# Experts' rows laid out in the order of work: input tiles of 128 rows that reach across experts, 22 and 21 instead of 32 and 32

## The chip, the core and the metric

One core of one Trainium2 chip runs the whole program. The metric is the device time in microseconds (us), a median over runs of one kernel. An expert's matrices are streamed from HBM for every use; nothing stays on the chip between the two layers.

## The reference, cut to what matters

The program is two transformer blocks of width 1024 on 1024 tokens. The change touches only the mixture of experts (MoE) that ends each of them. It is computed in float32:

```
logits -> one of 4 groups per token, then the top 2 of its 8 experts   # 2048 (token, expert) pairs
for each expert e, for its tokens x:
    y = (silu(x @ w_gate[e]) * (x @ w_up[e])) @ w_down[e]              # 1024 -> 512 -> 1024
out[token] += weight * y
```

There are 32 experts per layer, with 6 MB of weights each (gate, up and down of 2 MB).

## The kernel before

**Rooms.** How many tokens an expert gets is known only at run time, while the instructions are written beforehand. So the kernel ranks the experts by their counts on the chip and gives rank `r` a *room* of fixed size: `caps[r]` units of 32 rows, from a table `PROFILE`. Layer 0 has 88 units (2816 rows) in 31 rooms, layer 1 has 82 (2624 rows). What is over, and the expert of rank 31, goes through a small loop over 64 rows (`tensor_loop` and its likes; one pass of it runs here in each layer). `rooms(L)` makes the table of capacities and bases, from which VectorE works out each token's place (`vector_route`) and, through one-hot matmuls, the index table `xidx` that says which token lies in which row.

**Blocks.** A room is worked in blocks of 64 or 32 rows (`Plan.blocks`, in the order of `ORDER`). Layer 0 has 51, layer 1 has 46. For each block TensorE (PE) does gate and up together (L1914, eight steps over the contraction, the two in separate halves of the array's columns), the block before's hidden rows are turned (L1857), and the block before's down product follows (L1876). These stand in `tensor_experts.segment`.

**Tiles.** The rows that blocks read come in *tiles* of up to 128 rows (`Plan.tiles`). Per tile GpSimd (POOL) gathers the tokens' rows from HBM with one indirect DMA (`rows_in`, L1941), five tiles ahead (`XBUF = 5`); PE turns them with eight transposes (`turn`, L1846), VectorE (L1728) and ScalarE (L1800) copy them out of PSUM with four instructions each. The turn of the next tile stands in the middle of the first block of a tile:

```python
if off == 0 and t + 1 < tiles:
    turn(t + 1)
```

Before the change a tile covers rows of one room, or of two neighbouring rooms of odd size, so an expert with 64 rows has a tile of 64 rows for itself. Layer 0 then has 20 tiles of 64 rows and 12 of 128; layer 1 has 23 and 9. Gather slots without a token are marked as out of bounds and skipped.

**Weights.** The SyncE queue (SP) loads six pieces of 1 MB per expert (L2028, `sync_experts`) into 19 places (`homes`; 15 in layer 1). A piece waits until the block that used its place last is through. The loop's six pieces are issued between the experts, and the pieces that take over its places wait until the loop is done (`sync_loop_done`). The pieces' order and places depend only on rooms and blocks.

**Results.** Each block's product is written to `YE` in HBM (L1949). When all are through, `gpsimd_combine` gathers two rows of `YE` per token (L2178).

In the listing `Plan.__init__` builds order, blocks and tiles.

Of the kernel before, what the change touches and what calls it, by code (L numbers as in the profile page):

```python
# [27 lines left out]
def make_consts():  # L28
# [32 lines left out]
    for L in range(2):  # L61
        add(f"room{L}", rooms(L))
# [16 lines left out]

def rooms(L):  # L80

    r = np.arange(32)
    cap, base = np.full(32, 32), 32 * r
    for t in PROFILE[L]:
        cap, base = cap + 32 * (r < t), base + 32 * np.minimum(r, t)
    return np.concatenate([cap, base, 64 * (PLAN[L].places + 1) - cap - base])[None, :]


class Sig:


    def __init__(self, sem):
        self.sem, self.n = sem, 0
# [1506 lines left out]
Block = namedtuple("Block", "q at rows first tile off")  # L1600


class Plan:
# [1 line left out]


    def __init__(self, profile, firsts, before, homes):
        caps = [1 + sum(r < t for t in profile) for r in range(31)]
        base = [sum(caps[:r]) for r in range(31)]
        self.places = sum(caps) // 2  # L1610

        self.order, self.blocks, self.tiles, starts = [], [], [], []
        for r in firsts:
            g = [r, r + 1] if caps[r] % 2 else [r]
            assert base[r] % 2 == 0
            starts.append(len(self.order))
            at, end = base[r], base[g[-1]] + caps[g[-1]]
            t0 = len(self.tiles)
            self.tiles += [(u, 32 * min(4, end - u)) for u in range(at, end, 4)]
            for r in g:  # L1620
                u, e = base[r], base[r] + caps[r]
                while u < e:
                    n = 1 if u % 2 or e - u == 1 else 2
                    self.blocks.append(Block(len(self.order), u, 32 * n, u == base[r], t0 + (u - at) // 4,
                                             32 * ((u - at) % 4)))
                    u += n
                self.order.append(r)
        assert sorted(self.order) == list(range(31))
        self.ends = {}
        for n, row in enumerate(self.blocks):  # L1630
            self.ends[row.q] = n + 1
        self.loop_q = min(q for q in starts if q >= 26)
        self.b0, self.t0, self.w0 = (0, 0, [0] * HOMES) if before is None else (
            before.b0 + len(before.blocks), before.t0 + len(before.tiles), before.filled)
        self.place_pieces(homes)
# [38 lines left out]
PROFILE = ((23, 12, 6, 5, 5, 3, 3), (27, 11, 5, 3, 3, 1, 1))  # L1674
# [4 lines left out]
PLAN = [Plan(PROFILE[0], ORDER[0], None, HOMES_IN[0])]  # L1679
# [1531 lines left out]
```

How the kernel before makes its waits and increments, by code:

```python
def wait_sent(k, e, job):  # L246
    u, count = landed_by(job)
    e.wait_ge(k.s[f"d_sent{u}"].sem, count)
# [21 lines left out]
def vector_first_mods(k):  # L271
    V, s = k.nc.vector, k.s
    v, mod = mod_views(k), s["v_mod"]
    def rows(n):
        V.wait_ge(s["p_col"].sem, SUMS_DONE[n])
        got = k.ps[:, 4 + n, 0:128]
        if n == 0:
            V.wait_ge(s["d_gate"].sem, 128)
        if n < 2:
            V.tensor_tensor(v.rows[:, n, :], got, v.bias[:, n, :], ALU.add).then_inc(*mod.up())
            return
        V.scalar_tensor_tensor(v.rows[:, n, :], got, 1.0, v.bias[:, n, :], ALU.add, ALU.add).then_inc(*mod.up())
        V.wait_ge(mod.sem, mod.n)
        V.tensor_tensor(v.rows[:, n, :], v.rows[:, n, :], v.gain[:, n - 2, :], ALU.mult).then_inc(*mod.up())
    def columns(n):
        V.wait_ge(s["p_col"].sem, TURNS_DONE[n])
        V.tensor_copy((k.sh1, k.sc1)[n // 2][:, 4 * (n % 2):4 * (n % 2) + 4], k.ps[:, n, 0:128:32]).then_inc(*mod.up())
    rows(0)
    rows(1)
    columns(0)
    rows(2)
    columns(1)
    rows(3)
    columns(2)
    columns(3)
    V.wait_ge(mod.sem, COLUMNS_MADE)
    for h in range(2):
        for kk in range(5):
            x_ = k.hT[:, kk, 512 * h:512 * h + 512]
            i_ = V.tensor_scalar(x_, x_, k.sc1[:, kk:kk + 1], k.sh1[:, kk:kk + 1], ALU.mult, ALU.add)
        i_.then_inc(*mod.up())
    V.wait_ge(s["d_small"].sem, 112)
# [2 lines left out]
def scalar_first_mods(k):  # L308
    S, s = k.nc.scalar, k.s
    S.wait_ge(s["v_mod"].sem, COLUMNS_MADE)
    for h in range(2):
```

## Time and profile before

| | |
|---|---|
| median of 3 runs (lowest to highest) | 2941.55 us (2939.59 to 2944.01) |
| the profiled execution's own time | 2942.17 us |
| its span in the profile | 2941.0 us |
| MoE of layer 0, from its first matmul to its last | about 885 to 1455 us |
| MoE of layer 1 | about 2330 to 2891 us |

Two measures are read together. The busy time of PE says whether matmuls follow each other without a gap. The DMA share says whether the 16 DMA engines have work all the time; a share of about 1.0 means that the stream of weights can't go faster. Where PE is busy throughout and the DMA share falls below 1, the stream waits for PE to free places. The layer's weights are 192 pieces of 1 MB.

### The profile page before, as it was taken

The numbers are of one execution on the slowest core, as the hardware profiler recorded it, in microseconds if no ns is written. First come the engines' busy times: TensorE is split into PE (matmuls) and PEld (weight loads), VectorE is DVE, ScalarE is ACT, GpSimd is POOL, SyncE is SP. The second block draws the span as 40 slices with busy tenths as digits, with TensorE's granted clock in tenths as the row PEclk, the third lists the DMA queues.
The fourth block names the chain that finished last, engine by engine and source line by source line (L and its number), as shares of the span: only waits on it lengthen the run. The fifth ranks groups of instructions, "written<-read, shape, count | busy, mean of one in ns | idle before, by whom it ended". The sixth has DMA issues, their size and how long they took to land.

```text
span 2941.0 us, 36152 instructions
## 1 busy us (share of the span) xinstructions
PE 2657.5 (90%) x13778; PEld 1322.0 (45%) x13778; DVE 1128.0 (38%) x2869; ACT 670.2 (23%) x1612; POOL 394.2 (13%) x443
## 2 busy tenths in 40 slices
PE   5999999999968999999769998999899489999982
PEld 3466944444543344443335764555544334334431
DVE  3224927455251222222171114777843412222224
ACT  3115710000121111110050002656532211111111
POOL 1000000001001111111122111222610111111102
PEclk9999999999978999999879999999999799999996
DMA  8221014635149999998851111000000699999997
GB/s 304 114 79 58 2 51 164 200 129 200 38 179 389 403 389 359 399 395 348 327 202 47 43 43 29 30 30 30 15 31 29 240 397 388 383 361 372 358 413 292
DMA packets 207012, 607.57 MB, mean 207 GB/s; under 512 B 58928, under 2 KB 114488, under 8 KB 157560
## 3 DMA queue, kind: packets, MB, share of 16 engines
q1 hardware_dynamic: 150248, 540.17, 48.1%
q0 software_dynamic: 56592, 65.08, 6.7%
q8 instruction: 111, 1.82, 0.3%
q14 instruction: 61, 0.50, 0.0%
HBM read 559.24 MB, written 52.18 MB: 208 GB/s over the span
## 4 chain that ended last, share of the span: by engine, by line
PE 81%; DVE 7%; DMA 7%; issue 2%; SPq 2%; ACT 1%; POOL 0%; DVEq 0%; POOLq 0%; ACTq 0%
PE ps L1914 20%; PE ps L1876 9%; PE ps L1049 7%; PE ps L2577 6%; DMA R<-in_w_up 5%; PE ps L1370 4%; PE ps L543 4%; PE ps L1053 4%; PE ps L3077 3%; PE ps L2574 3%; PE ps L549 2%; PE ps L1846 2%; PE ps L1857 2%; PE ps L2852 2%; PE ps L855 1%
## 5 line engine op out<-in xcount | busy, mean ns | idle before, releaser
L1914 PE MATMUL ps<-R 128*64 128x512 f32 (+1 forms) x3480 | 645.6, 530 | 44.6 <-DMA R<-in_w_up 40.2
L1914 PEld LDWEIGHTS ps<-R 128*64 128x64 f32 (+1 forms) x3480 | 209.6, 129 | 332.3 <-issue 300.1
L1876 PE MATMUL ps<-R 128*64 128x512 f32 (+1 forms) x1744 | 278.1, 507 | 1.8 <-DVE R L1737 1.8
L1049 PE MATMUL ps<-R 128*128 128x512 f32 x512 | 225.6, 600 | 5.2 <-DMA R<-in_w_in 4.7
L1800 ACT ACTIVATE R<-ps,small 128x64 f32<-128x64 f32 (+1 forms) x256 | 87.0, 420 | 538.6 <-PE ps L1846 538.6
L1765 DVE TENSOR_TENSOR R<-ps,R 64x512 f32<-64x512 f32 (+1 forms) x97 | 59.9, 617 | 322.5 <-PE ps L1914 201.7
L1876 PEld LDWEIGHTS ps<-R 128*64 128x64 f32 (+1 forms) x1744 | 96.4, 126 | 168.2 <-issue 152.5
L1737 DVE COPY R<-ps 128x256 f32<-128x256 f32 (+1 forms) x97 | 38.0, 391 | 320.7 <-PE ps L1857 320.7
L1049 PEld LDWEIGHTS ps<-R 128*128 128x128 f32 x512 | 97.7, 192 | 129.0 <-issue 122.8
L1814 ACT ACTIVATE R<-ps 64x512 f32<-64x512 f32 (+1 forms) x97 | 52.4, 541 | 451.3 <-PE ps L1914 451.2
L1914 PE MATMUL ps<-XR,R 128*64 128x512 f32 (+1 forms) x392 | 132.2, 525 | 1.4 <-DVE R L1728 1.4
L1370 PE MATMUL ps<-R 128*128 128x512 f32 x256 | 113.5, 596 | 1.5 <-DVE R L1010 1.5
L3077 PE MATMUL ps<-R 128*128 128x512 f32 x256 | 113.7, 596 | 0.4 <-DVE R L2730 0.4
L543 PE MATMUL ps<-R 128*128 128x512 f32 x256 | 110.2, 592 | 0.0
L1949 POOL DMA_DIRECT2D YE<-R x49 | 39.7, 810 | 471.4 <-DVE R L1749 471.4
L1941 POOL DMA_INDIRECT R<-XN,xidx x52 | 53.6, 1030 | 342.6 <-DVE R L1522 324.2
L2577 PE MATMUL ps<-R 128*128 128x512 f32 x224 | 98.6, 592 | 0.0
L1728 DVE TENSOR_SCALAR R<-ps,small 128x64 f32<-128x64 f32 (+1 forms) x256 | 76.0, 359 | 40.8 <-PE ps L1846 40.0
L473 PE MATMUL ps<-cst,XR 128*128 128x128 f32 x256 | 38.0, 302 | 59.0 <-DVE XR L2267 35.0
L1026 ACT ACTIVATE XR<-ps 128x512 f32<-128x512 f32 x32 | 19.1, 597 | 305.3 <-PE ps L1049 305.3
L2852 PE MATMUL ps<-R,cst 128*128 128x512 f32 (+3 forms) x192 | 81.0, 504 | 1.2 <-DVE R L2767 1.2
L1857 PEld LDWEIGHTS ps<-cst,R 64*128 64x128 f32 x340 | 47.8, 208 | 69.4 <-issue 68.0
(376 smaller groups left out, 3973.9 us busy)
## 6 DMA issues: line engine op xcount, KB each, us to landing
R<-in_w_up SPq DMA_DIRECT2D x126, 1024.0 KB, 20.1
R<-in_w_down SPq DMA_DIRECT2D x117, 1024.0 KB, 21.9
R<-in_w_gate SPq DMA_DIRECT2D x107, 1024.0 KB, 22.2
R<-in_w_ada SPq DMA_DIRECT2D x40, 1024.0 KB, 5.5
XR<-in_w_gate SPq DMA_DIRECT2D x21, 1024.0 KB, 26.1
R<-in_w_in SPq DMA_DIRECT2D x7, 2048.0 KB, 13.6
R<-in_w_in SPq DMA_DIRECT2D x13, 1024.0 KB, 5.6
XR<-in_w_down SPq DMA_DIRECT2D x11, 1024.0 KB, 31.1
```

The source lines that it names most:

```text
L543: i_ = T.matmul(k.ps[:, b, :], wv[:, kk, 128 * a:128 * a + 128], toks, start=kk == 0, stop=kk == 7)
L1049: i_ = T.matmul(o, wv[:, kk, cols], k.hT[:, kk, tk], start=kk == 0, stop=kk == 7)
L1053: i_ = T.matmul(o, w4[:, g, cols], x4[:, g, tk], start=g == 0, stop=g == 3)
L1370: i_ = T.matmul(k.ps[:, n % 5, :], lhsT[:, m, 128 * i:128 * i + 128], wv[:, m, :], start=m == 0, stop=m == 7)
L1800: i_ = S.activation(v.xT[t % 2][:, 4 + kk, 0:n], k.ps[:, 3, 128 * kk:128 * kk + n], ACT.Identity, scale=scale[:, 4 + kk:5 + kk], bias=bias ...
L1857: i_ = T.transpose(k.ps[:, hidden_bank(b), 64 * kk:64 * kk + 64], h[:, kk, :], k.ident[0:64, 0:64])
L1876: i_ = T.matmul(k.ps[r * j:r * j + r, 5 + b % 2, 0:n], v.hT[b % 2][:, c:c + r], w[:, kk % 2, n * j:n * j + n], start=kk == 0, stop=kk == 3)
L1914: i_ = T.matmul(hidden_out(k.ps[P0 + r * j:P0 + r * j + r, b % 2, 0:n], r), x_, hidden_columns(w, r, j), start=kk == 0, stop=kk == 7)
L2574: i_ = T.matmul(o, right[:, kk, 128 * part.x:128 * part.x + 128], left[:, kk, :], start=first and kk == 0, stop=kk == 3, skip_group_check= ...
L2577: i_ = T.matmul(o, left[:, kk, :], right[:, kk, :], start=first and kk == 0, stop=kk == 3, skip_group_check=True)
L2852: i_ = T.matmul(z, k.C("nge"), lp[:, 0:N], start=False, stop=first and not diag, skip_group_check=True)
L3077: i_ = T.matmul(k.ps[:, mix_bank(n, a), :], v.oT[a][:, c, 128 * i:128 * i + 128], w[4 * a + c][:, 512 * h2:512 * h2 + 512], start=c == 0, ...
```

## The change

The bases of the rooms are no longer those of the ranks in a row, but those of the order in which the rooms are worked. So neighbours in time are neighbours in `xidx` as well, and a tile is simply the next 128 rows, across rooms. The cut is only at the loop: the rooms ahead of it are one run, those behind it another. Rooms, blocks, their order, the weights' order and places, the loop and the results' stores stay as they are, but for the addresses in `YE`.

```diff
@@ def rooms(L):
-    r = np.arange(32)
-    cap, base = np.full(32, 32), 32 * r
-    for t in PROFILE[L]:
-        cap, base = cap + 32 * (r < t), base + 32 * np.minimum(r, t)
+    P = PLAN[L]
+    cap = 32 * np.array(P.caps + [1])
+    base = 32 * np.array([P.base[r] for r in range(31)] + [2 * P.places])
@@ Plan.__init__
-        for r in firsts:
-            g = [r, r + 1] if caps[r] % 2 else [r]
...
-            at, end = base[r], base[g[-1]] + caps[g[-1]]
-            t0 = len(self.tiles)
-            self.tiles += [(u, 32 * min(4, end - u)) for u in range(at, end, 4)]
...
+        for begin, end in ((0, self.loop_q), (self.loop_q, 31)):
+            u0, t0 = at, len(self.tiles)
+            for q in range(begin, end):
+                r = self.order[q]
+                assert q not in starts or at % 2 == 0
+                self.base[r], u, at = at, at, at + caps[r]
+                while u < at:
+                    n = 1 if u % 2 or at - u == 1 else 2
+                    self.blocks.append(Block(q, u, 32 * n, u == self.base[r], t0 + (u - u0) // 4, 32 * ((u - u0) % 4)))
                     u += n
+            self.tiles += [(u, 32 * min(4, at - u)) for u in range(u0, at, 4)]
```

The change's lines are two fewer ahead of the experts' code, so L1846 of before is L1844 there, L1914 is L1912, L1941 is L1939.

**TensorE, a block in the middle of layer 0.** The block is the 27th of the layer (room 18, 64 rows); `R5` holds the turned rows, `R6` the hidden ones, `R1` the gathered ones, `R2` and `XR` weights. Before:

```order
L1914 MATMUL ps<-XR,R5 64x512
L1914 MATMUL ps<-R2,R5 64x512
L1857 MATMUL ps<-cst,R6 128x64 x4
L1846 MATMUL ps<-cst,R1 128x64 x8
L1914 MATMUL ps<-XR,R5 64x512
L1914 MATMUL ps<-R2,R5 64x512
```

The same block now:

```order
L1912 MATMUL ps<-XR,R5 64x512
L1912 MATMUL ps<-R2,R5 64x512
L1855 MATMUL ps<-cst,R6 128x64 x4
L1912 MATMUL ps<-XR,R5 64x512
L1912 MATMUL ps<-R2,R5 64x512
```

The turn of a tile of 64 rows is gone from this block; the block before it now turns a tile of 128 rows (`128x128 x8`) where it turned one of 64.

**GpSimd, the start of layer 0's MoE.** Each row is a DMA; the size is rows by columns gathered, and `L1968` is the loop's gather. Before:

```order
L1941 DMA R<-XN,xidx 64x1024 [waits v_rt,d_xn1,d_xn0]
L1941 DMA R<-XN,xidx 128x1024 x2
L1941 DMA R<-XN,xidx 64x1024
L1941 DMA g1b<-XN,xidx 64x1024
L1968 DMA R<-XN,xidx 64x1024
L1972 DMA SD<-cst 16x1x4
L1941 DMA R<-XN,xidx 64x1024 [waits p_xt]
L1949 DMA YE<-R 4x32x256 [waits v_yb]
L1941 DMA R<-XN,xidx 64x1024 [waits p_xt]
```

Now:

```order
L1939 DMA R<-XN,xidx 128x1024 [waits v_rt,d_xn1,d_xn0]
L1939 DMA R<-XN,xidx 128x1024 x3
L1939 DMA g1b<-XN,xidx 128x1024
L1966 DMA R<-XN,xidx 64x1024
L1970 DMA SD<-cst 16x1x4
L1939 DMA R<-XN,xidx 128x1024 [waits p_xt]
L1947 DMA YE<-R 4x32x256 [waits v_yb]
L1947 DMA YE<-acc 4x32x256 [waits v_yb]
L1939 DMA R<-XN,xidx 128x1024 [waits p_xt]
```

The five gathers ahead of the first block hold 640 slots where they held 448, and the sixth holds 128 where it held 64; the seventh stands one store later.

## Rows read from the trace of the kernel before

**Rows 1.** The page: busy time by engine; the chain that ended last, by engine.

```profile
PE 2657.5 (90%) x13778; PEld 1322.0 (45%) x13778; DVE 1128.0 (38%) x2869; ACT 670.2 (23%) x1612; POOL 394.2 (13%) x443
...
PE 81%; DVE 7%; DMA 7%; issue 2%; SPq 2%; ACT 1%; POOL 0%; DVEq 0%; POOLq 0%; ACTq 0%
```

**Rows 2.** Stretches: busy by engine (instructions), PE's granted clock, DMA share, GB/s.

```profile
911.00:1140.00 229.00, 229.00 (x1404) 91.24 (x1404) 50.62 (x115) 29.65 (x73) 29.12 (x33) 0.99 1.02 397
1145.00:1157.00 12.00, 12.00 (x58) 4.20 (x56) 1.80 (x3) 0.59 (x1) 0.86 (x1) 1.00 0.63 207
...
1341.00:1358.00 17.00, 17.00 (x132) 7.21 (x128) 4.02 (x9) 1.88 (x5) 1.63 (x2) 1.00 0.44 141
...
2373.00:2609.00 236.00, 228.29 (x1254) 91.95 (x1255) 52.23 (x120) 31.65 (x80) 31.90 (x35) 0.99 1.02 388
...
2637.00:2651.00 14.00, 14.00 (x72) 5.69 (x70) 3.32 (x8) 1.88 (x5) 1.24 (x2) 1.00 0.50 156
2651.00:2785.00 134.00, 134.00 (x910) 54.84 (x908) 30.59 (x71) 17.33 (x44) 18.51 (x21) 1.00 1.01 388
...
2790.00:2886.00 96.00, 80.09 (x443) 31.92 (x443) 17.35 (x44) 8.51 (x22) 6.76 (x9) 0.91 1.01 406
```

**Rows 3.** The chain in layer 0: start us, us, piece.

```profile
1082.26 0.89 PE ps L1846 x8
1083.15 3.58 PE ps L1914 x16
...
1094.22 3.58 PE ps L1914 x16
...
1190.04 3.58 PE ps L1914 x16
...
1201.11 1.09 PE ps L1846 x8
1202.20 3.58 PE ps L1914 x16
```

**Rows 4.** PE in time, layers 0 and 1, at waits: start us, us, [idle before].

```profile
910.77 4.53 PE L1914 MATMUL ps<-R 128*64 128x512 f32 x10 [9.71 <-DMA R<-in_w_up]
...
2373.10 5.35 PE L1914 MATMUL ps<-R 128*64 128x512 f32 x16 [4.43 <-DMA R<-in_w_up]
2518.55 3.65 PE L1914 MATMUL ps<-R 128*64 128x512 f32 x16 [0.58 <-DMA R<-in_w_up]
...
2608.96 5.48 PE L1914 MATMUL ps<-R 128*64 128x512 f32 x16 [6.10 <-DMA R<-in_w_up]
...
2868.76 3.56 PE L1914 MATMUL ps<-R 128*32 128x256 f32 x32 [2.35 <-DMA R<-in_w_up]
...
2884.62 2.02 PE L1914 MATMUL ps<-R 128*32 128x256 f32 x32 [1.42 <-DMA R<-in_w_up]
```

**Rows 5.** SP's DMA queue in time, around layer 1's loop.

```profile
2789.47 0.33 SPq L2028 DMA_DIRECT2D R<-in_w_gate  x1
...
2825.42 0.33 SPq L2028 DMA_DIRECT2D R<-in_w_up  x1
```

**Rows 6.** DMA queue of gathers and stores, 875 to 1457, then 2300 to 2897 us.

```profile
q0 software_dynamic: 25329, 20.08, 11.2%
...
q0 software_dynamic: 24304, 19.55, 10.9%
```

**Rows 7.** POOL in time, the first gather and the sixth tile's, layer 0.

```profile
876.46 1.27 POOL L1941 DMA_INDIRECT R<-XN,xidx  x1 [148.91 <-DVE R L1522]
...
886.73 0.99 POOL L1941 DMA_INDIRECT R<-XN,xidx  x1 [1.99 <-PE ps L1846]
```

**Rows 8.** VectorE's share of the copies in layer 0, by shape: busy us, mean ns.

```profile
L1728 DVE TENSOR_SCALAR R<-ps,small 128x64 f32<-128x64 f32 x80 | 22.0, 338 | 5.5 <-PE ps L1846 5.1
L1728 DVE TENSOR_SCALAR R<-ps,small 128x128 f32<-128x128 f32 x48 | 16.4, 404 | 15.0 <-PE ps L1846 15.0
```

**Rows 9.** A stretch at layer 0's first wait, columns as in rows 2.

```profile
906.00:916.00 10.00, 5.23 (x14) 1.72 (x16) 0.00 (x0) 0.00 (x0) 0.00 (x0) 0.50 1.02 376
```

More of the change, by code:

```diff
@@ L1607, in __init__ @@
     def __init__(self, profile, firsts, before, homes):
-        caps = [1 + sum(r < t for t in profile) for r in range(31)]
-        base = [sum(caps[:r]) for r in range(31)]
+        self.caps = caps = [1 + sum(r < t for t in profile) for r in range(31)]
         self.places = sum(caps) // 2
-        self.order, self.blocks, self.tiles, starts = [], [], [], []
-        for r in firsts:
-            g = [r, r + 1] if caps[r] % 2 else [r]
-            assert base[r] % 2 == 0
-            starts.append(len(self.order))
-            at, end = base[r], base[g[-1]] + caps[g[-1]]
-            t0 = len(self.tiles)
-            self.tiles += [(u, 32 * min(4, end - u)) for u in range(at, end, 4)]
[L1620 to L1625, printed above, removed]
+        groups = [[r, r + 1] if caps[r] % 2 else [r] for r in firsts]
+        self.order = [r for g in groups for r in g]
+        assert sorted(self.order) == list(range(31))
+        starts = [self.order.index(g[0]) for g in groups]
+        self.loop_q = min(q for q in starts if q >= 26)
+        self.base, self.blocks, self.tiles = {}, [], []
+        at = 0
+        for begin, end in ((0, self.loop_q), (self.loop_q, 31)):
[7 more added lines that the diff above has]
+                    self.blocks.append(Block(q, u, 32 * n, u == self.base[r], t0 + (u - u0) // 4, 32 * ((u - u0) % 4)))
                     u += n
-                self.order.append(r)
-        assert sorted(self.order) == list(range(31))
+            self.tiles += [(u, 32 * min(4, at - u)) for u in range(u0, at, 4)]
         self.ends = {}
@@ L1631, in __init__ @@
             self.ends[row.q] = n + 1
-        self.loop_q = min(q for q in starts if q >= 26)
         self.b0, self.t0, self.w0 = (0, 0, [0] * HOMES) if before is None else (
```

## The prediction

> **What bounds the kernel now.** I read the page first: PE is busy 90% of the span and makes 81% of the chain that ended last [rows 1]. A turn saved on PE can therefore be worth its time, but only where PE sets the pace, so the MoE stages have to be cut into stretches [rows 2]. The reader should hold two columns against each other. In layer 0, from 911 to 1140 us, PE is busy for all 229 us and the DMA engines are at 1.02 as well. Who leads shows where one of them lets go: from 1145 to 1157 and from 1341 to 1358 the DMA share falls to 0.63 and 0.44 while PE stays fully busy. The stream had filled every place and waited for PE. After the first wait, PE never waits for a weight in layer 0. So layer 0 is PE's from 910.77 us on, and before that it is the stream's: PE stands 9.71 us for a weight [rows 4].
>
> Layer 1 has three parts. Up to 2608.96 us the DMA share is 1.02 without a break, and PE is busy for 228.29 of 236 us [rows 2]; it waits for weights at 2373.10, 2518.55 and 2608.96, the last time for 6.10 us [rows 4]. There the stream leads. From 2609 to 2789 PE leads: it is never idle, and the share drops to 0.50 between 2637 and 2651 [rows 2]. Then SP issues pieces again from 2789.47 on [rows 5], the share is 1.01 to the end of the stage, and PE waits at 2868.76 and 2884.62 [rows 2, 4]. The tail is the stream's, but its start hangs on PE at 2789.
>
> **What goes from PE.** A turn costs what it adds to the distance between two like places of the chain. From 1083.15 to 1094.22 no turn lies between: 11.07 us. From 1190.04 to 1202.20 lies a turn of 128 rows: 12.16, so 1.09 us, which is also the length of the piece itself; the turn of 64 rows ahead of 1083.15 takes 0.89 [rows 3]. Twice the rows cost 1.22 times as much, so merging pays.
>
> *Layer 0.* After 910.77 us, 30 turns are left of the 32: 19 of 64 rows and 11 of 128, which is 19 x 0.89 + 11 x 1.09 = 28.9 us. Now 20 of 128 are left of 22: 21.8 us. **-7.1 us.** The first two turns, before and after, lie ahead of the weights' wait of 9.71 us and are worth nothing either way.
>
> *Layer 1.* What is saved before 2609 only lengthens the waits at 2518 and 2609. From there to 2789 there are 10 turns (6 of 64, 4 of 128: 9.7 us); now 7 (1 of 64, 6 of 128: 7.4 us). **-2.3 us**, which SP's issues after 2789.47 inherit and with them the whole tail. The four turns behind the loop become two (3.6 to 2.2 us); the waits at 2868 and 2884 absorb that.
>
> A rule of the skill speaks against all this. In the Trainium skill, "TensorE: Matmul & The Clock Gate", section "Back-to-back issue gap", the gap follows the moving columns: about 60 cycles for up to 64, 134 for 128. By that ratio of 2.2 a turn of 128 rows would cost 1.99 us beside 0.89, layer 0 would have 19 x 0.89 + 11 x 1.99 = 38.8 us before and 39.8 after, and the change would lose 1 us there. The trace's 0.89 and 1.09 [rows 3] disagree with it (its figures are for bf16), and the sum goes by the trace.
>
> **What it adds.** *Wider copies.* VectorE's four copies per tile take 404 ns each instead of 338 [rows 8]. They hide behind half a block, except at the first tile behind the loop, where PE waits for them: 4 x 66 ns = **+0.3 us** in layer 0; in layer 1 the tail's waits hide it.
>
> *Rows fetched earlier.* No slot is added over a layer, but five tiles of lookahead are 640 slots now. By the first weights' wait in layer 0, six tiles hold 768 slots instead of 512, and a seventh of 64 was issued at about 903 before: 192 to 256 slots more. How many carry a row? q0 moved 20.08 MB in layer 0 [rows 6]; 2816 + 64 stored rows of 4 KB are 11.8, so 8.3 MB or some 2020 rows were gathered from 2816 slots, 0.72. In layer 1 it is 19.55 - 11.0 = 8.5 MB from 2624 slots, 0.79. So 140 to 185 rows, 0.57 to 0.75 MB, go ahead of weights on engines that are full (share 1.02); at the 397 GB/s of rows 2 that is 1.4 to 1.9 us. I take **+1.7 us** for layer 0. The gathers are issued from 876 to 887 us [rows 7], in time to be ahead of the pieces that PE waits for at 910. The bounds are 0, if those pieces are ahead in their own queue anyway, and 256 full rows, 2.6 us. In layer 1, when the piece of 2608.96 is under way, the gathers stand at about tile 15 (1920 to 2048 slots) instead of 20 or 21 (1728 to 1792): some 220 x 0.79 = 170 rows more, 1.8 us at 388 GB/s. I take **+1.7 us**, bounds 0 and 2.7. Those rows are then missing from the traffic later; of them the last tile's (64 slots, about 50 rows) fell about 2780 to 2800, and without it the tail is **-0.5 us**.
>
> The Trainium skill, "DMA: Bandwidth & Descriptors", section "Queues, rings and completion order", says that each DMA engine takes packets from its queues in turn, so gathered rows do cut in ahead of queued weights. By that the upper part of the bounds applies; no row here shows the order of single packets.
>
> *Nothing else.* Table entries change, not the instructions that make them. A gather costs POOL about 1 us [rows 7]; there are 21 fewer. The gather of the tile five ahead still stands behind a wait for a turn, and the stores of results are queued behind it on POOL; that turn comes in the same block as before, so nothing is held longer. At the start the first tile lands later, since more of its slots carry rows; the 9.71 us that PE then waits anyway cover it.
>
> **The sum.** Layer 0: -7.1 + 0.3 + 1.7 = -5.1. Layer 1: -2.3 + 1.7 - 0.5 = -1.1. Together -6.2 us against the profiled execution's 2942.17 (span 2941.0 and 1.2 around it). That execution lies 0.6 us above the median of 2941.55, so the forecast for the median is 2941.55 - 6.2 = **2935.4 us**. A change of 0.2% (5.9 us) is about what a measurement of this kernel tells from none.
>
> **The rivals.**
> *The head start is free.* If the early rows ride beside the weights, both +1.7 vanish and the sum is -9.6: 2932. For it: q0 needs only 11% of the engines [rows 6]. Against it: the share is 1.02, so nothing is free. Chance 0.17.
> *The stream takes more back.* PE gets nearer to the stream in layer 0 as well. From 911 to 1140 PE gains about 3 us on a stream that is full all the time, and after 2651 it does so for 134 us. If new waits for weights eat half of the 7.1 and the 2.3, and the head start costs 2.6 and 2.7, the sum is -4.7 + 0.3 + 5.3 - 0.5 = +0.4: 2942. For it: the share of 1.01 to 1.02. Against: the idle stream at 1145 and 1341, which shows some us of slack. Chance 0.23.
> *The turn is priced by columns* (the rule above). With 1.99 us for a turn of 128 rows layer 0 gives +1.0 in place of -7.1; from 2609 to 2789 it is 6 x 0.89 + 4 x 1.99 = 13.3 us before and 0.89 + 6 x 1.99 = 12.8 now, so -0.5. With the other terms: 1.0 + 0.3 + 1.7 - 0.5 + 1.7 - 0.5 = +3.7, 2945. Rows 3 speak against it. Chance 0.02.
> *Slower: the clock.* At a wait PE's granted clock falls to the 1.2 GHz level: from 906 to 916 it is 0.50 [rows 9], with the wait of 9.71 us just before it [rows 4]. Work in such a stretch of 10 us takes 5 us longer. The waits at 910, 2373, 2518 and 2609 get longer. If each of two that PE's own part follows (910 and 2609) brings one such stretch more, that is +10 and 2945; with a third it is +15 and 2950. This case decides for slower when more than 6.2 + 5.9 = 12.1 us are lost, so from the third stretch on. Against it: the waits change by 2 us or less. Chance 0.08 for one stretch or more.
>
> **The numbers.** The forecast itself has a chance of 0.5, with a range of its own from 2933 to 2938. The range over all cases reaches down past the free head start and up past the stream's case: 2930.5 to 2943; some 0.07 lie below and 0.1 above. Faster by over 0.2% (below 2935.7) are 0.17 of the free head start and a little over half of the forecast's own case, 0.28, whose middle lies just under that bound, with 0.02 of the rest: 0.47. Slower by over 0.2% (above 2947.4) is most of the clock's case, 0.06. Within it: 0.47.
>
> **What the profile will show.** PE has 21 turns fewer, 168 transposes. If the theory is right, blocks without a turn stay 11.07 us apart and those with one are 12.16; no wait for a weight shows in layer 0 behind the first; the first waits end 1 to 2 us later than 910.77 and 2373.10; layer 0's MoE ends about 5 us earlier; and the wait at 2608.96 gets 1 to 2 us longer. The prediction is wrong if eight transposes of 128 rows take over 1.5 us, if waits for weights stand between 911 and the loop of layer 0, if the tail of layer 1 ends no earlier although SP's issues of 2789.47 do, or if a stretch of clock 0.50 shows that was not there.

## The result, and the profile after

The changed kernel takes **2912.84 us** (median of 4 runs, 2910.02 to 2918.0), beside 2942.78 us for the kernel before on the same chip (4 runs, 2939.59 to 2945.34). The ratio is 0.9901, with a 95% interval from 0.9883 to 0.9918: about 30 us less. The forecast was 2935.4 us with a range of 2930.5 to 2943. The time lies 18 us below that range.

The page of the profiled execution (span 2916.8 us, the slowest of the four runs), first the lines that answer to [rows 1], then the DMA queues:

```profile
PE 2643.1 (91%) x13610; PEld 1307.0 (45%) x13610; DVE 1110.6 (38%) x2785; ACT 648.3 (22%) x1528; POOL 374.1 (13%) x422
...
q1 hardware_dynamic: 150248, 540.17, 47.4%
q0 software_dynamic: 56256, 65.07, 6.5%
...
PE 81%; DVE 7%; DMA 6%; issue 2%; SPq 1%; ACT 1%; POOL 0%; DVEq 0%; POOLq 0%; ACTq 0%
```

The same two queues on the page of the kernel before (packets, MB, share of 16 engines over a span of 2941.0 us):

```profile
q1 hardware_dynamic: 150248, 540.17, 48.1%
q0 software_dynamic: 56592, 65.08, 6.7%
```

PE's busy time falls by 14.4 us (2657.5 to 2643.1) with 168 instructions fewer: 21 turns of eight transposes. That part was foreseen. The other part was not: q1, which holds the weights, moves the same 150248 packets and the same 540.17 MB, but in 47.4% of 2916.8 us (1382.6) instead of 48.1% of 2941.0 (1414.6). **The same packets took 32 us less of engine time.** A share is printed to 0.1%, so this is good to some 3 us.

Stretches after, columns as in [rows 2]:

```profile
911.00:1140.00 229.00, 229.00 (x1392) 89.66 (x1390) 48.15 (x103) 25.46 (x58) 27.52 (x31) 0.99 1.02 407
1145.00:1157.00 12.00, 12.00 (x60) 4.19 (x56) 1.80 (x3) 0.59 (x1) 0.86 (x1) 1.00 0.59 201
...
2360.00:2584.00 224.00, 224.00 (x1212) 86.06 (x1208) 47.62 (x99) 26.55 (x60) 25.14 (x28) 0.99 1.01 404
```

In layer 1, from its fourth block to the one at which the lead passed to PE (2609 before, 2584 now), the engines moved 388 GB/s before at a DMA share of 1.02 [rows 2]; now they move 404 at 1.01. The share was at its top both times and the rate was not. And PE, which was busy for 228.29 of 236 us there, is now busy for all 224.

PE in time at its waits for rows and weights, to be read against [rows 4]; the first line, the wait for the first tile's rows, answers to the 9.87 us of before:

```profile
887.59 1.97 PE L1844 MATMUL ps<-cst,R 128*128 128x128 f32 x8 [10.32 <-DMA R<-XN,xidx]
...
909.94 5.39 PE L1912 MATMUL ps<-R 128*64 128x512 f32 x12 [5.95 <-DMA R<-in_w_up]
...
2344.17 6.13 PE L1912 MATMUL ps<-R 128*64 128x512 f32 x16 [6.58 <-DMA R<-in_w_up]
...
2359.56 2.83 PE L1912 MATMUL ps<-R 128*64 128x512 f32 x6 [3.42 <-DMA R<-in_w_up]
...
2589.86 3.65 PE L1912 MATMUL ps<-R 128*64 128x512 f32 x16 [1.36 <-DMA R<-in_w_up]
...
2853.00 3.64 PE L1912 MATMUL ps<-R 128*32 128x256 f32 x32 [4.96 <-DMA R<-in_w_up]
```

The wait of 0.58 us at the block of 2518.55 is gone, and that of 6.10 us at 2608.96 too: the same block starts at 2584.24 without one. Over the program, the view of who waits for whom gives, first for before and then for after:

```profile
PE ps L1914 <- DMA R<-in_w_up: 40.2, 12, 9.7
```

```profile
PE ps L1912 <- DMA R<-in_w_up: 29.4, 9, 6.6
```

So 14.4 us less work on PE and 10.8 us less waiting for weights are 25.2 us, and the two profiled spans differ by 24.2. The turns themselves are as read before: blocks without one between them stay 11.08 us apart (1162.94 to 1174.02), and with one 12.16:

```profile
1162.94 3.58 PE ps L1912 x16
...
1174.02 3.58 PE ps L1912 x16
...
1185.09 1.09 PE ps L1844 x8
1186.18 3.58 PE ps L1912 x16
```

The time between like places, each less the same of before. The places are the first gate matmuls of the blocks that started at 910.8 (layer 0), 1447.8 (its last block), 2609.0 and 2789.5 (layer 1) before, and layer 1's first table matmul (2318.4). A second profile of the changed kernel (a0, below) stands beside it, since one profile scatters by some us:

| stretch | forecast | profile after | a0 |
|---|---|---|---|
| up to the end of layer 0's first wait for weights | +1.7 | -0.8 | -2.0 |
| from there to layer 0's last block | -6.8 | -9.9 | -10.2 |
| to layer 1's table | 0 | +0.6 | -0.5 |
| to the block of 2609 (weights led before) | +1.7 | **-14.6** | **-15.0** |
| to the block of 2789.5 (PE led) | -2.3 | -2.6 | -2.6 |
| to the end | -0.5 | +3.1 | -0.6 |
| sum | -6.2 | -24.2 | -30.9 |

Half of what came (15.0 of 30.9 us in a0) or more (14.6 of 24.2) lies in the one stretch in which nothing was to be gained. How far single profiles scatter is seen in e1 below, which does the same work as before and takes as long: its stretches differ from those of before by -1.3, -4.0, -0.1, +1.0, +0.8 and -1.5 us. So the second row is good to some 4 us, and the fourth stands far outside.

### The profile page after: what moved, and what is told of

Read it like the earlier page. It is cut to its first block, busy times and chain, and to the rows that moved or that the text cites. A ratio compares the mean times of both kernels' runs of the same rounds, so it can differ in the third digit from the quotient of the medians.

```text
span 2916.8 us, 35522 instructions
## 1 busy us (share of the span) xinstructions
PE 2643.1 (91%) x13610; PEld 1307.0 (45%) x13610; DVE 1110.6 (38%) x2785; ACT 648.3 (22%) x1528; POOL 374.1 (13%) x422
## 3 DMA queue, kind: packets, MB, share of 16 engines
q1 hardware_dynamic: 150248, 540.17, 47.4%
## 4 chain that ended last, share of the span: by engine, by line
PE 81%; DVE 7%; DMA 6%; issue 2%; SPq 1%; ACT 1%; POOL 0%; DVEq 0%; POOLq 0%; ACTq 0%
PE ps L1912 20%; PE ps L1874 9%; PE ps L1048 7%; PE ps L2575 6%; PE ps L1369 4%; PE ps L542 4%; DMA R<-in_w_up 4%; PE ps L1052 4%; PE ps L3075 3%; PE ps L2572 3%; PE ps L548 2%; PE ps L1855 2%; PE ps L2850 2%; PE ps L1844 1%; PE ps L854 1%
## 5 line engine op out<-in xcount | busy, mean ns | idle before, releaser
L1912 PE MATMUL ps<-R 128*64 128x512 f32 (+1 forms) x3480 | 641.5, 529 | 34.5 <-DMA R<-in_w_up 29.4
L1912 PEld LDWEIGHTS ps<-R 128*64 128x64 f32 (+1 forms) x3480 | 207.9, 129 | 321.8 <-issue 291.2
L1048 PEld LDWEIGHTS ps<-R 128*128 128x128 f32 x512 | 97.7, 192 | 129.2 <-issue 123.1
L1798 ACT ACTIVATE R<-ps,small 128x128 f32<-128x128 f32 (+1 forms) x172 | 64.7, 457 | 357.5 <-PE ps L1844 357.5
L1912 PE MATMUL ps<-XR,R 128*64 128x512 f32 (+1 forms) x392 | 130.6, 521 | 1.6 <-DVE R L1726 1.6
L1939 POOL DMA_INDIRECT R<-XN,xidx x35 | 37.8, 1081 | 341.3 <-DVE R L1521 325.3
L542 PEld LDWEIGHTS ps<-R 128*128 128x128 f32 x256 | 48.6, 190 | 61.2 <-issue 61.2
```

The lines of the kernel that those rows point to most:

```text
L542: i_ = T.matmul(k.ps[:, b, :], wv[:, kk, 128 * a:128 * a + 128], toks, start=kk == 0, stop=kk == 7)
L1048: i_ = T.matmul(o, wv[:, kk, cols], k.hT[:, kk, tk], start=kk == 0, stop=kk == 7)
L1798: i_ = S.activation(v.xT[t % 2][:, 4 + kk, 0:n], k.ps[:, 3, 128 * kk:128 * kk + n], ACT.Identity, scale=scale[:, 4 + kk:5 + kk], bias=bias ...
L1912: i_ = T.matmul(hidden_out(k.ps[P0 + r * j:P0 + r * j + r, b % 2, 0:n], r), x_, hidden_columns(w, r, j), start=kk == 0, stop=kk == 7)
```

## The experiments

**The theory.** The kernel before fetched 43 of its 64 tiles by gathers of 64 slots, which land in 64 of the 128 partitions; now one of 43 is. (The loop's own gather of 64 slots, one a layer, is the same in all kernels and not counted.) Such a gather slows the weights' packets that land beside it, a gather of 128 slots does not. **The rivals:** the new addresses do it; or TensorE's fewer turns do it alone, on the path.

Every kernel ran beside the kernel before on the same chip, and a ratio is to that. 2938.76 us was the time of before beside e1, e2, e3 and e5, 2940.68 beside a0, e4 and e6, and 2938.81 beside e7, e8 and e9.

### e1: the layout alone

The kernel before with the new addresses of the rooms, but its own 32 tiles a layer and its own gathers:

```
-    r = np.arange(32)
-    cap, base = np.full(32, 32), 32 * r
+    cap = 32 * np.array(P.caps + [1])
+    base = 32 * np.array([P.base[r] for r in range(31)] + [2 * P.places])
...
+                if q in starts:
+                    u0, t0 = at, len(self.tiles)
+                    over = at + sum(caps[x] for x in groups[starts.index(q)])
+                    self.tiles += [(u, 32 * min(4, over - u)) for u in range(u0, over, 4)]
```

> The rooms lie in the order of work as in the changed kernel, but tiles are cut per room as before: 32 and 32 tiles, 20 and 23 of them with gathers of 64 slots. Theory (a gather of 64 slots slows the weights' packets while it lands; one of 128 doesn't): as before, 2942 us within 0.2%, mean duration of a weights' packet in layer 1 about 334 ns as before. Rival (the new addresses in the index table and in the results' buffer make it faster): 2913 us.

2939.32 us, ratio 0.9999 (0.9989 to 1.0009). The addresses alone bring nothing that shows, and that rival is out.

### e2: the gathers alone

The kernel before, each tile of 64 rows fetched by a gather of 128 slots. The upper 64 slots' indices lie outside the table, so no row lands for them; some small VectorE instructions a layer write these indices.

```
-        at, n = P.tiles[t]
+        at, n = P.tiles[t][0], 128
...
+    up, got, n = k.xidx[64:128, :], k.ps[64:128, 1, :], PLAN[L].places
...
+    settle(V.tensor_scalar(up[:, 0:n], got[:, 0:n], 0.0, 3.0 * NO_ROW, ALU.mult, ALU.add))
+    for u in [u // 2 for u, n in PLAN[L].tiles if n == 128]:
+        V.tensor_scalar(up[:, u:u + 1], got[:, u:u + 1], float(NO_ROW), None, ALU.add).then_inc(*rt.up())
```

> The kernel before, with the same 32 and 32 tiles, turns and blocks, but every gather has 128 slots: where the tile has 64 rows, the upper 64 slots are marked out of bounds, so that the same rows move in the same number of DMAs. Theory (the gather's shape): the slow packets go, weights' packets at about 318 ns; 15 to 25 us less than before, so 2917 to 2927 us. Rival (fewer gathers, or fewer turns on TensorE, make the whole gain): as before, 2942 us.

2930.35 us, ratio 0.9965 (0.9953 to 0.9977): 8.4 us less, about half of what was expected, although the queue of weights gained all of it. The rows of those 43 tiles still land in partitions 0 to 63 alone, so the landing place by itself did not slow the stream; a gather of 64 slots did. Its line on the page (span 2930.8):

```profile
q1 hardware_dynamic: 150248, 540.17, 47.1%
```

That is 1380.4 us, as in the changed kernel. Its stretch of layer 1 shows where the rest went:

```profile
2373.00:2600.00 227.00, 226.15 (x1248) 89.81 (x1246) 52.16 (x120) 31.86 (x80) 30.83 (x33) 0.99 0.99 392
```

PE is busy for 226.15 of 227 us, and the DMA share is below 1 (0.99): the stream has room, and PE, which still makes all its turns, is what holds the stretch up. By the places of the table above, e2 gains 8.3 us in the stretch up to the block of 2609, where the stream led, and 0.3 us from layer 0's first wait to its last block, where PE leads. A faster stream alone is worth its time only up to where PE becomes the bound.

### e3, e4, e9: the turns alone, with more and fewer gathers of 64 slots

The changed kernel, its TensorE instructions untouched, with tiles of 128 rows fetched by two gathers of 64 slots: all of them (e3), every second one (e4), and every second one from the sixth on (e9). Shown is e4, cut; e3 has no `t % 2 == 1`, e9 has `and t > 4` behind it.

```
-        G.indirect_dma_start(v.xb[t % XBUF][0:n], None, k.XN[L],
-                             bass.IndirectOffsetOnAxis(ap=k.xidx[0:n, at // 2:at // 2 + 1], axis=0),
+        parts = [(0, 64), (64, n)] if n == 128 and t % 2 == 1 else [(0, n)]
+        for lo, hi in parts:
+            G.indirect_dma_start(v.xb[t % XBUF][lo:hi], None, k.XN[L],
+                                 bass.IndirectOffsetOnAxis(ap=k.xidx[0:hi - lo, (at + lo // 32) // 2:(at + lo // 32) // 2 + 1],
...
```

> The changed kernel with every tile of 128 rows fetched by two gathers of 64 slots, one into partitions 0 to 63 and one into 64 to 127; the turns stay those of the changed kernel. Theory (the shape): 44 and 41 such gathers where the kernel before had 20 and 23, each some 0.9 us of the stream: the stream leads everywhere, slower than the kernel before by 5 to 20 us, 2947 to 2962 us. Rival (fewer turns on TensorE make the gain): about 2913 us.

> The changed kernel, but every second tile of 128 rows is fetched by two gathers of 64 slots instead of one of 128 (22 gathers of 64 and 11 of 128 in layer 0, 21 of 64 and 10 of 128 in layer 1). TensorE's instructions are exactly those of the changed kernel, and the number of gathers of 64 slots is about that of the kernel before (20 a layer). Theory (a gather of 64 slots slows the weights' packets that land beside it, one of 128 does not; the turns alone are worth what the prediction said): 6 to 9 us faster than the kernel before, 17 to 20 us slower than the changed kernel. Rival (TensorE's fewer and wider turns bring the gain, or fewer rows of descriptors in all): as the changed kernel, about 26 us faster than before.

> The changed kernel, with tiles 5, 7, 9, ... of each layer fetched by two gathers of 64 slots, so that the five tiles ahead of the first weights stay whole: 35 gathers of 64 slots in the program instead of 1. If each costs the end time 0.75 us as in the other two, 25 us more than the changed kernel (about 2939). If a large part of the cost lies in the tiles ahead of the first weights (block 2 of layer 0 came 5 to 7 us later with them split), 12 to 16 us more.

| kernel | gathers of 64 slots for tiles | median us | ratio to before | q1's engine time, us (share x span) |
|---|---|---|---|---|
| changed | 1 | 2912.84 | 0.990 | 1382.6 |
| e9 | 35 | 2937.66 | 0.9994 (0.9984 to 1.0003) | 1415.9 (48.3% x 2931.5) |
| e4 | 43 | 2945.04 | 1.0016 (1.0006 to 1.0026) | 1422.2 (48.3% x 2944.6) |
| e3 | 85 | 2978.39 | 1.0139 (1.0116 to 1.0162) | 1455.3 (48.9% x 2976.1) |
| before | 43 | 2938.8 | 1 | 1414.6 |
| e2 | 0 | 2930.35 | 0.9965 | 1380.4 (47.1% x 2930.8) |

```profile
q1 hardware_dynamic: 150248, 540.17, 48.9%
...
q1 hardware_dynamic: 150248, 540.17, 48.3%
```

That is e3's line, then that of e4, which e9's page has too. The packets and bytes are those of before in each of them. Against a0, the changed kernel as it ran beside e4 (2913.5 us), e3's 84 more gathers cost 64.9 us, e4's 42 cost 31.5, e9's 34 cost 24.1: 0.77, 0.75 and 0.71 us of the end time each. The kernel before was 1.9 us faster beside e3 and e9 than beside a0, so their two prices may be some hundredths low. The rival is out, since TensorE's work is the same in all four. e3 was expected at 2947 to 2962 and came out at 2978; e4 was to be 6 to 9 us faster than before and is 4.4 slower; e9 came near the 2939 of its first case. The two misses have one side: in the changed kernel PE is so near to the stream that a slower stream is paid nearly in full (in e3 q1 takes 72.7 us more and the end comes 64.9 us later). The stretch of layer 1 in e3, over the same 224 us as the last row of after:

```profile
2360.00:2584.00 224.00, 194.25 (x1114) 75.96 (x1104) 39.93 (x85) 21.59 (x49) 29.92 (x33) 0.93 1.02 366
```

366 GB/s at a share of 1.02, and PE stands for 30 us. In e4 the saved turns are seen where PE leads (6.8 us less from layer 0's first wait to its last block, which is the forecast's term, though by one profile, good to some 4 us), but layer 0's block of 910.8 starts 5.2 us later, and the stretch up to the block of 2609 takes 4.6 us longer. e9 leaves the tiles ahead of the first weights whole, where e4 fetches tiles 1 and 3 by pairs of gathers, and its block is not late. That block in e4, then in e9:

```profile
915.94 4.53 PE L1912 MATMUL ps<-R 128*64 128x512 f32 x10 [11.55 <-DMA R<-in_w_up]
...
907.62 5.23 PE L1912 MATMUL ps<-R 128*64 128x512 f32 x16 [8.24 <-DMA R<-in_w_up]
```

### m1: the stream by itself

No part of the model: SP loads 252 pieces of 1 MB, and in six of seven phases POOL adds the same 0.52 MB of rows for every three pieces, in another form each time. It leaves out all computation, and its output is copied weights. It ran once.

```
g64       i_ = gather(x, 0, 64, ng % 4)          # twice
g128      i_ = gather(x, 0, 128, 4 + ng % 4)     # once
g128_low  i_ = gather(x, 0, 128, 8 + ng % 4)     # twice, upper 64 indices out of bounds
p64       i_ = G.dma_start(X[x][0:64, :], rows[64 * (ng % 16):64 * (ng % 16) + 64, :])      # twice
p128      i_ = G.dma_start(X[x][:, :], rows[128 * (ng % 8):128 * (ng % 8) + 128, :])        # once
g64_up    i_ = gather(x, 64, 64, ng % 4)         # twice
```

> No part of the model: a stream of weight pieces of 1 MB alone, in seven phases of 36 pieces, in which other transfers land beside it: none; two gathers of 64 slots for every three pieces; one gather of 128 slots; two gathers of 128 slots with the upper half of the slots out of bounds; two plain loads of 64 partitions; one plain load of 128 partitions; two gathers of 64 slots into partitions 64 to 127. Each gather of 64 slots is 0.25 MB of rows. Theory (what lands in 64 partitions only, lands through part of the ports and holds the weights' packets up): the phases with 64 partitions, gathers and plain loads alike, take 1.5 us more for each pair than the same bytes in 128 partitions; the phases with 128 slots take what their bytes need at the stream's own rate. Rival (it is a property of gathers, or of the out of bounds slots, not of the number of partitions): the plain loads of 64 and 128 partitions take the same. Rival (it needs TensorE's or VectorE's work beside it): no phase differs from its bytes.

Stretches inside the phases none, g64, g128, g128_low, p64, p128, g64_up (the last two columns are DMA share and GB/s):

```profile
20.00:75.00 55.00, 0.00 (x0) 0.00 (x0) 1.00 1.01 422
100.00:204.00 104.00, 0.00 (x0) 16.88 (x19) 1.00 1.02 343
212.00:308.00 96.00, 0.00 (x0) 10.87 (x11) 1.00 1.01 420
318.00:426.00 108.00, 0.00 (x0) 21.76 (x22) 1.00 1.00 393
440.00:560.00 120.00, 0.00 (x0) 11.20 (x22) 1.00 1.02 324
575.00:666.00 91.00, 0.00 (x0) 5.28 (x10) 1.00 1.01 419
684.00:800.00 116.00, 0.00 (x0) 18.68 (x20) 1.00 1.02 329
```

A transfer of 128 partitions leaves the rate at 419 to 422 GB/s, and two of 64 in its place take it down to 324 to 343, gather or plain load, lower half or upper. g128_low stands between (393), though its rows land in partitions 0 to 63 as those of g64 do. The share says 1.00 to 1.02 in all seven. POOL's issues follow the landing of every third piece, so their distance is the time for 3 pieces and 0.52 MB (3.67 MB in all, 8.7 us at 422 GB/s):

```profile
76.97 1.05 POOL L35 DMA_INDIRECT X<-in_x,idx  x1 [76.52 <-DMA W<-in_w_gate]
...
204.79 1.00 POOL L35 DMA_INDIRECT X<-in_x,idx  x1 [9.39 <-DMA W<-in_w_gate]
...
309.47 0.99 POOL L35 DMA_INDIRECT X<-in_x,idx  x1 [7.74 <-DMA W<-in_w_gate]
```

In g64 the twelve periods from 76.97 to 204.79 take 10.65 us each, in g128 those to 309.47 take 8.72. In the same way p64 takes 11.46, p128 8.79, g64_up 11.02 and g128_low 9.87. A transfer of 64 partitions thus costs the stream 0.97 us (gather, lower half), 1.15 (upper) or 1.33 (plain load, against p128) above its bytes. The rival that it needs work on other engines is out, and so is the one that it is a property of gathers. Slots out of bounds are a half cure here: such a gather still costs 0.6 us.

The packets in the traces show that this remainder is another thing. Each piece of weights comes as 128 packets of 8 KB, which take 314 ns on average with nothing beside them. Of them 35% take over 400 ns in g64, 36% in g64_up and 29% in p64, but none in the phase without rows and one of 4215 in g128. In g128_low none does from 318 to 366 us, and over the whole stretch it is 3%. So neither rows that land in half of the partitions nor two gathers in place of one hold the weights' packets up as 64 slots do. In the kernels the same count, of 49280 such packets, is 2678 before, 6677 in e3, 492 after and 546 in e2. How the packets of a transfer of 64 differ otherwise, and what the 0.6 us of g128_low are, no trace here shows.

The Trainium skill, "SBUF — State Buffer", section "Door 1: The DMA port swizzle", says that partitions 0 to 63 are reached through 8 of 16 ports only, and 64 to 127 through the other 8. The direction agrees with 343 against 420 GB/s and with the upper half behaving as the lower. As an estimate from that page, 0.262 MB at half of 420 GB/s take 1.25 us instead of 0.62, so 0.6 us more. The transfers of 64 partitions show 0.97 to 1.33, and the measurement decides. The halves alone do not explain them, since the rows of g128_low and e2 land in the same half. No run shows a port, so that the ports have a part in it is argued and not shown.

### e5: what a turn is worth now

The changed kernel, with the eight transposes of every third tile made twice: 15 turns more.

```
-            for kk in range(4):
+            for kk in 2 * list(range(4)) if t % 3 == 0 else range(4):
```

> The changed kernel, with every third tile turned twice (the second turn repeats the first), 7 x 1.09 = 7.6 us of TensorE's work more in layer 0 behind the first wait and 3.3 us more in the last part of layer 1: TensorE's time as before, gathers as in the changed kernel. Theory (TensorE's part as predicted, the rest of the gain is the stream's): 2921 to 2925 us, 8 to 11 more than the changed kernel. Rival (the whole gain is the stream's): 2913 us; rival (the whole gain is TensorE's): 2942 us.

2925.92 us, ratio 0.9956 (0.9937 to 0.9975), 12 to 13 us more than the changed kernel, a little above the 8 to 11 that were expected. Two of the 15 stand ahead of waits for the first weights; the other 13 cost 0.95 us each, near the 1.09 that a turn lasts. With the fast stream PE's time counts nearly everywhere, in layer 1 too: the stretch up to the block of 2609 takes 2.8 us longer than in the changed kernel's profile. So both rivals of e5, that the whole gain is the stream's or TensorE's, are out.

### e6, e7, e8 and a0: fewer rows fetched ahead

```
-XBUF, YBUF = 5, 6
+XBUF, YBUF = 3, 6        # e6, e7; 2 in e8
...
-        at, n = P.tiles[t]
+        at, n = P.tiles[t][0], 128        # e7 and e8: the last gather of 64 slots too
```

> The changed kernel with three buffers of gathered rows instead of five, so that three tiles instead of five are fetched at the start of a layer, ahead of or beside the first weights. The prediction took 1.7 us a layer for the rows that are fetched earlier. If that holds: 2 to 3 us faster than the changed kernel, and layer 1's first gate matmul 1 to 2 us earlier after its layer's start. Rival (these rows land beside the weights at no cost, since they come by gathers of 128 slots): as the changed kernel within 1 us; slower than it, if three buffers are too few and a tile's rows come late.

> The changed kernel itself, for comparison with the others on the same chip: 0.990 of the kernel before, as measured.

> The changed kernel with three buffers of rows, and layer 1's last tile of 64 rows fetched by a gather of 128 slots as well, so that no tile is fetched by 64 slots. Theory: that gather costs about 0.75 us of the end time as all others did (64.9 us for 84 of them, 31.5 us for 42), so 0.5 to 1 us less than with three buffers alone, 6 us less than the changed kernel. Rival: no difference from three buffers alone, since TensorE is the bound by then.

> The same with two buffers of rows. Theory (each tile fetched ahead of the first weights delays them by its bytes, 0.5 MB or 1.2 us): up to 1 us a layer less than with three. Rival: a tile's rows are asked for only when the tile two before it has been turned, and its turn waits for them: 1 us or more at many of 43 tiles, some 10 us and more in all.

a0, the changed kernel again: 2913.53 us, ratio 0.9912 (0.9895 to 0.9928). e6: **2908.05 us**, 0.9894 (0.9878 to 0.9911), 5.5 us below a0. The intervals of the two ratios overlap; the runs themselves hardly do (2907.05 to 2911.49 beside 2911.27 to 2915.97), so a gain of some us is likely and its size is not sure. Its first weights are there earlier; PE at both layers' first waits:

```profile
905.41 5.35 PE L1912 MATMUL ps<-R 128*64 128x512 f32 x16 [3.99 <-DMA R<-in_w_up]
...
2335.50 5.35 PE L1912 MATMUL ps<-R 128*64 128x512 f32 x16 [4.00 <-DMA R<-in_w_up]
```

905.41 beside 908.8 (a0) and 909.94 (after), so 3.4 to 4.5 us earlier; in layer 1, counted from its first table matmul, 2.7 us earlier than in a0. Two tiles of 128 slots are at most 1.05 MB, 2.6 us at 407 GB/s, so rows fetched ahead do cost their bytes or somewhat more: the prediction's term for a head start has the right kind. e7 (2909.72 us, 0.9894) shows no further gain from the last gather, whose 0.75 us lie below what four runs can tell. e8 (2910.23 us, 0.9886, 0.9866 to 0.9906) scatters from 2904.09 to 2915.68; the 10 us that its rival expected did not come, and whether two buffers are better or worse than three stays open. The best kernels of the study are thus the changed one with two or three buffers of rows, about 1.1% below before.

## Why the prediction was wrong

**The step that failed** is the reading of the DMA share. "There the stream leads" was right for layer 1 up to 2609, but the prediction took a share of 1.02 as a stream that cannot go faster (so it stands under "Time and profile before" too, and it is wrong), and priced the rows as bytes on it. It looked for a change of bytes (+1.7, +1.7, -0.5) and never asked at what rate they land. [rows 2] held the hint: 397 and 388 GB/s at 1.02, but 406 at 1.01 in the last stretch. The share counts the time in which a packet is under way, and a packet that is held up counts for longer. m1 shows 343 GB/s at 1.02 and 422 at 1.01, and e3 has 366 at 1.02 where after has 404 at 1.01. The gathers were counted ("there are 21 fewer", a cost on POOL only) and their slots too, but not how many slots one gather has.

**"What is saved before 2609 only lengthens the waits"** followed from it and fell with it: the turns were put at nothing there, and +1.7 us was added. That stretch gave 14.6 to 15.0 us: the stream became faster (e2 has 8.3 us of it with the turns of before), and so the turns saved on PE, which would have been worthless, counted as well. Neither part does much alone: the wide gathers without the turns bring 8.4 us (e2), the turns with 35 or 43 gathers of 64 slots bring 1.2 us, no more than the scatter, or lose 4.4 (e9, e4). Together they bring 27 to 30.

**Term by term.** Layer 0's turns: -7.1 forecast. e4, in which the stream is as burdened as before, shows -6.8 from the first wait to the last block, and the changed kernel -9.9 to -10.2; e1, with the turns of before, has -4.0 by scatter alone, so the term stands within what single profiles tell, and its price of 1.09 us and its count were right. Wider copies: 403 ns now beside the 404 of [rows 8], too small to be seen in the end. Rows fetched earlier: the first wait ends 0.8 to 2.0 us earlier and not 1.7 later. e6 shows that the bytes do cost at least what was said; that the faster landing of the weights outweighs them is read from the GB/s ahead of that wait's end, 360 before and 414 now (columns as in [rows 2]).

```profile
888.00:911.00 23.00, 12.96 (x172) 7.58 (x166) 2.92 (x8) 3.55 (x7) 1.74 (x2) 0.80 1.02 360
...
888.00:910.00 22.00, 14.32 (x180) 8.13 (x179) 4.28 (x12) 5.06 (x11) 1.83 (x2) 0.81 1.02 414
```

Layer 1's turns from 2609 to 2789: -2.3 forecast, -2.6 measured in both profiles. The tail: -0.5 forecast, +3.1 in one profile and -0.6 in the other, so no more than the scatter of single executions.

**The rivals.** A free head start (0.17) had the right sign and not the mechanism. The stream taking more back (0.23) was the opposite of what came: no wait for a weight shows in layer 0 behind the first. The turn priced by columns (0.02) and the clock (0.08) did not show: a turn of 128 rows is 1.09 us, and the clock is 0.99 in both long stretches. None of them had the stream gaining speed, and this is why the range missed.

**What stays open.** Why e4 has 7.6 us more of q1's engine time than before with the same 43 gathers, and e9 1.3 more with 35; pairs of gathers back to back, where before had single ones, are a guess that no run tests. And what it is in a transfer of 64 partitions that holds the weights' packets up, since a gather of 128 slots with the upper half out of bounds puts its rows in the same place and does not.

## What to carry to other kernels

A DMA share of 1.0 says that packets fill the engines' time, not that the stream is at its best: read the GB/s beside it, over several stretches, and ask of every small transfer that lands beside a stream how many partitions it is issued over. Here each gather of 64 slots cost about 0.75 us of the end where PE was near to the stream, and in m1 one of 128 cost nothing beyond its bytes. And where two resources are near each other, price a change that relieves both as one: each half alone may be worth almost nothing.

## What the runs showed of the hardware

- Two loads or gathers of 64 partitions per 3 MB of a stream of 1 MB pieces, in place of one of 128, take the total from 420 to between 324 and 343 GB/s, for the same bytes; lower and upper half are near each other (343 and 329), and a plain load is worse than a gather (1.33 against 0.97 us each). The share stays at 1.02.
- A gather of 128 slots of which 64 are out of bounds costs the stream 0.6 us in m1, between the two, but hardly lengthens the weights' packets (3% over 400 ns, beside 35%); in e2, q1's engine time was that of the changed kernel (1380.4 beside 1382.6 us).
- The same 540.17 MB of weights took from 1380 to 1455 us of engine time as the number of gathers of 64 slots for tiles went from 0 to 85: 0.88 us each.
